# Asking for two expert weight chunks before the first gathered rows are in

## What is computed

```python
def hier_moe(h, w_rg, b_rg, w_re, b_re, w_gate, w_up, w_down):
    g_logits = (h @ w_rg) + b_rg                      # 4 groups: the best one
    ...                                               # 8 experts in it: the best two
    order = jnp.argsort(eid)
    xs = h[order // TOP_K_IN_GROUP]                   # each expert's tokens, gathered
    sizes = jnp.bincount(eid, length=N_EXPERTS)
    a = lax.ragged_dot(xs, w_gate, sizes)
    u = lax.ragged_dot(xs, w_up, sizes)
    ys = lax.ragged_dot(jax.nn.silu(a) * u, w_down, sizes)
    y = jnp.zeros_like(ys).at[order].set(ys).reshape(T, TOP_K_IN_GROUP, D)
    return jnp.einsum('tkd,tk->td', y, w.astype(y.dtype))
```

## Time and profile before

| | us |
|---|---|
| median of 3 runs | 1416.78 |
| lowest and highest of them | 1416.59 to 1417.98 |
| the profiled execution | 1419.13 |
| its span on the core | 1417.3 |
| TensorE busy in the span | 1385.1 (98%) |
| VectorE busy | 913.1 (64%) |
| ScalarE busy | 654.7 (46%) |
| moved by DMA | 235.27 MB, mean 166 GB/s |

### The profile page before, as it was taken

The page is one execution under the profiler, slowest core; times in us unless marked ns, Lnnn a source line. Parts: engine busy times, 40 slices in busy tenths (PEclk is TensorE's granted clock), DMA queues, the critical chain, the costliest instruction groups (busy, mean ns, idle before and its releaser), DMA issues. The chain is left out here.

```text
span 1417.3 us, 18812 instructions
## 1 busy us (share of the span) xinstructions
PE 1385.1 (98%) x7503; PEld 1147.0 (81%) x7503; DVE 913.1 (64%) x1275; ACT 654.7 (46%) x863; POOL 78.5 (6%) x71
## 2 busy tenths in 40 slices
PE   9999999999999999999999999997999999999997
PEld 7788878877888888888878888886888888777886
DVE  6730366657886676555564443348899999888574
ACT  7321222212333432433351121244888888888565
POOL 0000000000000000000000000003122122211000
PEclk9999999999999999999999999998999999999999
DMA  9300111015443622233253346316999999995231
GB/s 332 115 0 1 52 31 31 16 42 163 124 123 100 268 60 60 75 104 114 95 166 104 104 122 243 134 74 226 371 384 381 391 387 388 373 376 225 102 136 46
DMA packets 119433, 235.27 MB, mean 166 GB/s; under 512 B 14128, under 2 KB 78256, under 8 KB 104752
## 3 DMA queue, kind: packets, MB, share of 16 engines
q1 hardware_dynamic: 108800, 212.79, 42.5%
q0 software_dynamic: 9248, 16.80, 3.2%
q10 hardware_dynamic: 1296, 4.46, 0.8%
HBM read 204.64 MB, written 41.94 MB: 174 GB/s over the span
## 5 line engine op out<-in xcount | busy, mean ns | idle before, releaser
L1874 DVE TENSOR_TENSOR two_chunk_lo<-two_chunk_raw,two_hi 128x2048 fp32r<-128x2048 f32 x96 | 217.4, 2287 | 22.7 <-ACT two_hi L1870 22.5
L1870 ACT CAST two_hi<-two_chunk_raw 128x2048 fp32r<-128x2048 f32 x96 | 181.2, 1918 | 10.9 <-DMA two_chunk_raw<-w_e 9.7
L3115 PE MATMUL two_banks<-two_hi,two_xT_hi 128*128 128x512 f32 x256 | 102.6, 401 | 1.0 <-DVE two_xT_lo L2298 1.0
L3117 PE MATMUL two_banks<-two_hi,two_xT_lo 128*128 128x512 f32 x256 | 100.1, 391 | 0.0
L3116 PE MATMUL two_banks<-two_chunk_lo,two_xT_hi 128*128 128x512 f32 x256 | 99.9, 390 | 0.0
L1558 ACT CAST mix_w_hi<-mix_w_raw 128x512 fp32r<-128x512 f32 x72 | 44.7, 621 | 104.3 <-DVE mix_w_raw L1666 55.8
L1671 DVE TENSOR_TENSOR mix_w_lo<-mix_w_raw,mix_w_hi 128x512 fp32r<-128x512 f32 x72 | 49.6, 689 | 45.8 <-ACT mix_w_hi L1558 45.1
L2978 PE MATMUL two_banks<-mix_y_hi,mix_w_hi 128*128 128x512 f32 x192 | 74.8, 389 | 2.2 <-PEq L146 2.2
L1784 PE MATMUL front_sums<-two_T_hi,mix_w_hi 128*128 128x512 f32 x192 | 75.3, 392 | 0.0
L1786 PE MATMUL front_sums<-two_T_hi,mix_w_lo 128*128 128x512 f32 x192 | 74.9, 390 | 0.0
L1785 PE MATMUL front_sums<-two_T_lo,mix_w_hi 128*128 128x512 f32 x192 | 74.7, 389 | 0.0
(11 more groups left out here) (385 smaller groups left out, 3337.0 us busy)
## 6 DMA issues: line engine op xcount, KB each, us to landing
two_chunk_raw<-w_e SPq DMA_DIRECT2D x102, 1024.0 KB
mix_w_raw<-w_in SPq DMA_DIRECT2D x44, 512.0 KB, 3.9
quarter_sums<-two_T_buf_lo SPq DMA_DIRECT2D x32, 256.0 KB, 2.5
sigs<-two_staged SPq DMA_DIRECT2D x8, 1024.0 KB, 4.5
two_sig<-sigs SPq DMA_DIRECT2D x16, 512.0 KB, 4.5
two_r<-results SPq DMA_DIRECT2D x16, 512.0 KB, 4.9
heads_values<-x SPq DMA_DIRECT2D x8, 512.0 KB, 9.6
vals_w_raw<-w_in SPq DMA_DIRECT2D x8, 512.0 KB, 7.0
```

The costliest lines, as they stand in the source:

```text
L1870: self.nc.scalar.copy(self.high(n)[:], self.raw(n)[:]).then_inc(self.hi_ok, 1)
L1874: self.nc.vector.tensor_tensor(self.low(n)[:], self.raw(n)[:], self.high(n)[:].bitcast(F32), ALU.subtract).then_inc(self.lo_ok, 1)
L3115: nc.tensor.matmul(sums, xT_hi[u][:, k, :], hi[:, cols], start=(k == 0), stop=False)
L3117: mm = nc.tensor.matmul(sums, xT_lo[u][:, k, :], hi[:, cols], start=False, stop=(k == last))
```

## The change

SP no longer waits for the gathered rows of the first two experts before it asks for chunks 9 and 10. The two waits ahead, for the slots, stay.

```diff
             chunks.load(sp, dram, 8)
             sp.wait_ge(slots_ok, 1)
             sp.wait_ge(slots_mm, 2)
-            for e in range(2):
-                sp.wait_ge(gathered[e], 16)
             for n in (9, 10):
                 chunks.load(sp, dram, n)
             for n in range(SLOTS, CHUNKS + FINALS):
```

## The result

| | before | after |
|---|---|---|
| median, us | 1416.78 | 1421.73 |
| lowest and highest | 1414.54 to 1419.32 | 1417.75 to 1424.17 |
| the profiled execution | 1419.13 | 1421.69 |
| its span | 1417.3 | 1419.8 |

Both medians are of 13 executions. The ratio is 1.0033, with 95% between 1.0025 and 1.004: the change makes the kernel slower, by 4.95 us as the difference of the medians (3.5 to 5.7 by the ends of the interval). That is 2.4 us more than forecast and 0.4 us above the upper end of the range.

A forecast was written before the change was run, and what follows sets the result against it. It took TensorE to bound the stage up to about 1204 and the stream of chunks to 1255. Landing 2.4 plus clock 2.2, less the stream's gain 2.1, gave 2.5 us over 1416.78: 1419.3 us, range 1415.2 to 1421.3.

The forecast's parts named there:

- D: TensorE's lateness after the first gather: 2.4 us from the later landing plus 2.2 us from the clock, 4.6 us together.
- The first landing: Before TensorE's first turn: the first gather, now with two more chunks ahead, lands 2.4 us later, at 988.9.
- another gather's 7.9 us: Issue to landing of the gather issued at 985.79, beside chunks 9 and 10; taken as the first gather's new time.
- the third rival: At the first gather: it waits until the chunks ahead have passed, landing 4.0 us late; time 1420.9 us, chance 0.20.
- The granted clock: TensorE after its 3.9 us gap: it runs at 1.2 GHz from 988.9 to about 995, costing 2.2 us.
- The first two rivals: Around the first gather: clock stays up, 1417.1 us, chance 0.20; or gather not delayed, 1414.7 us, chance 0.14.
- the fourth: At SP's requests: something else holds chunks 9 and 10, so the change does nothing; chance 0.02.
- b: Gain of the chunk stream near 990 from asking for chunks 9 and 10 sooner: 2.1 us, bounds 1.1 and 3.8.
- the queue is empty at 993.2: DMA from 982: three chunks and five gathers, 4.46 MB, move at 400 GB/s in 11.2 us, ending at 993.2.
- the new idle time: DMA engines between the emptied queue and chunk 11, which waits for TensorE: 0.25 us plus TensorE's lateness.
- the old one: Idle DMA time from 984.5 to 989.5 in the kernel before, at share 0.53: 2.35 us, to be filled by chunks.
- the forecast's own count: Stream of chunks: new DMA idle time less the old 2.35 us moves its end by TensorE's lateness less 2.1 us.

The follow-up runs named there:

- the second pair: One further profiled execution each of the unchanged kernel before and the unchanged changed kernel: 1417.94 us before, 1424.97 us after.
- e5: The kernel before with chunk 9 alone asked for ahead of the two waits for gathered rows: 4.06 us slower than before, ratio 1.003.
- e9: The kernel before with chunk 8 too asked for only after the first gathered rows: 1.20 us slower than before, ratio 1.001.
- e6: The changed kernel with 36 products without use ahead of the first turn, not 18, and 4 behind it: 3.19 us slower than before, ratio 1.0023.
- e11: The kernel before with 41 products without use in place of 18, making TensorE late: 3.44 us slower than before, ratio 1.002.
- e3: The kernel before with the filled slots dealt evenly over the partitions: 3.22 us faster than before, ratio 0.9966.
- e4: The changed kernel with the filled slots dealt evenly over the partitions: 1.55 us slower than the kernel before, ratio 1.0011.
- e2: The changed kernel with 38 products without use in place of 18: 3.94 us slower than the kernel before, ratio 1.0028.

## Why the prediction was right in its direction and short in size

**Right: the place, and D.** The first landing was on the path, nothing hid its delay, and it was 3.0 us (3.6 in the second pair) where 2.4 was forecast, within its bounds of 0 to 3.7. It was sized from another gather's 7.9 us; e5 and e9 show that the delay grows with the chunks ahead, as in the third rival, where the forecast took one size for it. The idle time before the first turn was 4.4 us for a forecast of 3.9. The granted clock fell to 0.50 and stayed there for 7.0 us from the first turn on, 986.97 to 994, for a forecast of 6.1. It cost 2.4 us for a forecast of 2.2. So D was 5.4 to 6.1 us, and 4.6 was expected; the second gather stayed hidden, as was said. The first two rivals, a clock that stays up and a gather that isn't delayed, are out, and so is the fourth, that the change does nothing.

**Wrong: b, the gain of the stream.** It was put at 2.1 us, with bounds of 1.1 and 3.8. Measured, it is 0.6 and -1.6 by the stalls of the two pairs of profiles, 0.3 by e6 against e11, and 0.4 to 1.1 as D less the 4.95 us of the medians. None is above the lower bound of 1.1, though each is known to 1 or 2 us only. The rest of the error, 0.8 to 1.5 us, is D, larger than its 4.6. In b two steps failed.

The first is the line "4.46 MB, at 400 GB/s 11.2 us: the queue is empty at 993.2". 400 GB/s holds for chunks. The gathers took what the chunks left over, and what then remained of them went at 84 to 150 GB/s, with the mean share at 0.35 from 987 to 992. Only four gathers were queued there, too, since the fifth waits for the first turn. The earlier trace rows had the warning: 143 GB/s at a share of 0.53, in a stretch in which gathers were in flight. I read the missing 0.47 as time without requests. It was mostly the rate of the gathers themselves. So the new idle time, put at 0.25 + D = 4.85 us, came out at 8.8, and the old one at 3.3 where 2.35 was taken.

These two numbers come from the forecast's own count, done on the two traces from G + 1 to G + 49. The kernel before, besides the stretch of 0.53 in the earlier trace rows:

```profile
982.00:984.50 2.50, 2.50 (x11) 2.04 (x10) 2.43 (x3) 0.00 (x0) 1.90 (x2) 0.86 0.93 375
...
989.50:999.50 10.00, 9.07 (x46) 7.25 (x45) 5.47 (x4) 6.54 (x6) 0.99 (x1) 1.00 0.97 373
999.50:1009.50 10.00, 10.00 (x51) 8.32 (x50) 9.29 (x15) 6.91 (x7) 0.99 (x1) 1.00 0.99 372
1009.50:1030.00 20.50, 20.50 (x103) 17.01 (x102) 19.02 (x15) 17.32 (x19) 4.01 (x4) 1.00 0.98 369
```

And the kernel after, behind 987:

```profile
987.00:997.00 10.00, 9.45 (x36) 7.67 (x37) 4.11 (x4) 2.73 (x4) 1.83 (x2) 0.66 0.36 117
997.00:1007.00 10.00, 9.07 (x45) 7.28 (x45) 7.51 (x13) 6.49 (x8) 0.52 (x2) 1.00 0.86 316
1007.00:1027.50 20.50, 20.50 (x103) 17.05 (x102) 18.56 (x15) 18.00 (x18) 4.51 (x5) 1.00 0.96 359
```

Before: 0.2 + 2.35 + 0.3 + 0.1 + 0.4 = 3.3 us idle (the 2.35 from the earlier trace rows). After: 0.2 up to 987, then 6.4 + 1.4 + 0.8, together 8.8. The difference is 5.5 us, which is D - b, and with D = 5.4 it leaves b = 0 (rounded). So the form of the count was right, and the term for the new gap was sized 4 us too small (0.8 us of it through D). The count can't say why, though: chunks from 11 on are asked for as TensorE frees them, so a late TensorE leaves engines idle by itself.

The second step is the balance over 16 engines: I took idle time of the mean engine for time in which chunks could have moved to an earlier end. e3 shows that the uneven load made the stalls, as they are gone altogether with it spread. That the idle time near 987 lay on the engines that the end of the stream doesn't hang on is inferred from this; no record here tells the engines apart. The prediction named this as the likeliest way to be wrong, and gave its size, "up to 4.6 us"; it should have been a case with a chance and a price of its own, not a closing remark. The range ended at 1421.3, and b was never allowed under 1.1: with b = 0 the forecast's own D of 4.6 gives 1421.4.

**Open.** From G to the turn of 28 experts later the changed kernel needs 290.66 and 291.84 us, the kernel before 285.85 and 284.22: 6.2 more on the mean, while the medians say 4.95. Between e4 and e3 it is 6.35 us by the traces, 4.77 by the medians and 6.4 by the ratios. G was 0.8 to 3.0 us earlier in the changed kernel in these pairs, but the change can't move G by any path that the trace shows. Whether that is chance was not settled. No run delays the first gather with no chunk in flight, which would price the landing apart from the chunks. The nearest is e11, which has the lateness without the early chunks, and it costs nearly what e6 costs. Whether b is a small gain or a small loss stays open.

## What to carry to other kernels

A transfer that someone is waiting for should have as little as possible asked for ahead of it: here each further 1 MB chunk cost the first gather 1 to 2 us, and the gap made by two or three of them cost the clock as well. Before counting idle DMA time as a gain, ask which engines were idle: a mean share near 0.5 beside a half-filled gather may be half of the engines at their limit, and spreading the gather shows whether it is. Where an indirect transfer fills only part of its partitions, spreading the filled ones gave more (3.2 us) than any order of the requests.

## What the runs showed of the hardware that was not expected

- The landing of the first gather against the chunks asked for ahead of it: 4.3 us with none, 4.9 to 5.5 with one, 7.4 with two, 8.4 to 9.4 with three. With the filled slots spread: 3.2 with none, 4.3 with one, 8.1 with three.
- Packed gathers left alone moved 84 GB/s at 25% of the engines (after, 989 to 994 us) and some 130 at 38% (before, 985 to 988), where chunks moved at some 400. Spread ones held 75% for a microsecond (e3).
- The clock fell after two gaps of 0.99 and 0.96 us, with 10.6 us of products ahead of them (e2), and did not fall after 1.53 and 0.96 us with 6.2 us of products ahead (before). Filling both gaps (0.33 us left before the turn) kept it at 1.00 (e6).
- Dealing the filled slots of gathers and scatters over all partitions took all waits for chunks out of the stage (9.7 us of them before) and made the kernel 3.2 us faster by the medians.
